# A decoder layer with 32 experts on one core: one expert's weights go where the residual rows lay, and the embedding rows take a way through memory

## What is computed

```
mix = (sigmoid(ga) * branch_a + sigmoid(gb) * branch_b) @ w_out
x = layer_norm(DN_ALPHA * x + mix, ln1_g, ln1_b)
ffn = hier_moe(x)          # best of 4 groups, 2 best of its 8 experts; SwiGLU experts
x = layer_norm(DN_ALPHA * x + ffn, ln2_g, ln2_b)
ple = sigmoid(x @ w_ple_gate) * (p @ w_ple_proj)
x = x + rms_norm(ple, ple_norm_g)
```

## Time and profile before

| what | us |
|---|---|
| median of 3 runs | 960.75 |
| lowest, highest | 960.75, 961.34 |
| profiled execution | 960.12 |
| its span | 958.3 |

### The profile page before, as it was taken

One profiled execution on the slowest core, in us unless ns is written; L12 is line 12 of the kernel. 1 busy time (PEld: TensorE's weight loads), 2 busy tenths in 40 slices (PEclk: granted clock), 3 DMA queues, 4 the chain that ended last, 5 costly groups with the idle time before them and its releaser, 6 DMA issues.

```text
span 958.3 us, 14059 instructions
## 1 busy us (share of the span) xinstructions
PE 918.7 (96%) x5317; PEld 553.9 (58%) x5317; DVE 425.0 (44%) x979; ACT 249.0 (26%) x538; POOL 96.8 (10%) x146
## 2 busy tenths in 40 slices
PE   8999999999999999999999999989999889987997
PEld 7777777777777766565678744444333323333444
DVE  0311467767734228777642243682111211113784
ACT  1122222032145015566740011131111101111346
POOL 0111211211221200000000000011121111110000
PEclk9999999999999999999999999999999999999999
DMA  9876888998797802011024794349999999998601
GB/s 374 346 250 233 283 289 316 328 334 302 275 349 273 291 23 69 28 39 42 21 80 154 307 425 171 150 164 345 419 423 423 421 427 423 424 418 352 250 23 66
DMA packets 65418, 247.52 MB, mean 258 GB/s; under 512 B 11301, under 2 KB 12078, under 8 KB 56358
## 3 DMA queue, kind: packets, MB, share of 16 engines
q1 hardware_dynamic: 46742, 191.41, 51.4%
q0 software_dynamic: 13216, 35.28, 10.1%
q10 hardware_dynamic: 5392, 19.93, 5.6%
HBM read 240.98 MB, written 18.05 MB: 270 GB/s over the span
## 4 chain that ended last, share of the span: by engine, by line
PE 76%; DMA 12%; DVE 6%; ACT 2%; issue 2%; SPq 1%; DVEq 0%; ACTq 0%
PE ps L895 21%; DMA arena<-in_wexp 10%; PE ps L1365 8%; PE ps L1285 6%; PE ps L1216 4%; PE ps L1490 3%; PE ps L1387 3%; PE ps L983 3%; PE ps L954 3%; PE ps L1068 3%; PE ps L886 3%; PE ps L1092 2%; PE ps L1032 2%; PE ps L1049 1%; PE ps L958 1%
## 5 line engine op out<-in xcount | busy, mean ns | idle before, releaser
L895 PE MATMUL ps<-arena 128*128 128x260 f32 x928 | 214.3, 386 | 1.7 <-DMA arena<-in_xT 1.4
L895 PEld LDWEIGHTS ps<-arena 128*128 128x128 f32 x928 | 172.7, 190 | 36.7 <-issue 8.8
L1874 DVE SCALAR_TENSOR_TENSOR arena<-arena,vec 128x512 f32<-128x512 f32 x120 | 81.7, 745 | 0.0
L2556 POOL DMA_DIRECT2D arena<-in_kv x96 | 51.7, 539 | 264.4 <-issue 258.3
L1387 PE MATMUL ps<-arena 128*64 128x512 f32 x288 | 67.8, 614 | 5.3 <-DMA arena<-in_wexp 5.3
L1365 PE MATMUL ps<-arena 128*64 128x512 f32 x288 | 65.4, 607 | 6.9 <-DMA arena<-in_wexp 5.8
L1365 PE MATMUL ps<-arena,con 128*64 128x512 f32 x288 | 63.8, 595 | 2.9 <-DMA arena<-in_wexp 2.9
L2381 DVE TENSOR_TENSOR arena<-ps,arena 128x256 f32<-128x256 f32 x18 | 7.6, 424 | 125.4 <-ACT arena L1725 125.4
L1285 PE MATMUL ps<-arena 128*128 128x512 f32 x128 | 58.0, 600 | 0.0
L1387 PEld LDWEIGHTS ps<-arena 128*64 128x64 f32 x288 | 22.1, 142 | 48.3 <-issue 48.3
L1216 PE MATMUL ps<-arena 128*128 128x260 f32 x224 | 49.3, 382 | 0.0
(11 more groups left out here) (360 smaller groups left out, 1196.4 us busy)
## 6 DMA issues: line engine op xcount, KB each, us to landing
arena<-in_wexp SPq DMA_DIRECT2D x26, 2048.0 KB, 25.2
arena<-in_kv SPq DMA_DIRECT2D x160, 272.0 KB, 9.2
arena<-in_wexp SPq DMA_DIRECT2D x36, 1024.0 KB, 27.3
arena<-in_kv POOLq DMA_DIRECT2D x96, 272.0 KB, 7.5
arena<-in_w ACTq DMA_DIRECT2D x35, 512.0 KB, 7.3
arena<-in_wexp SPq DMA_DIRECT2D x16, 512.0 KB, 9.5
arena<-in_wo SPq DMA_DIRECT2D x8, 512.0 KB, 3.3
arena<-in_w_out SPq DMA_DIRECT2D x4, 1024.0 KB
```

The source lines that it names most:

```text
L895: y = mm(ps[:, b + h, 0:TH], w[:, k], xT[:, k, h * TH:(h + 1) * TH], start=(k == 0), stop=(k == KD - 1))
L1874: y = v.scalar_tensor_tensor(out=aT[:, c, 0:NPR], in0=win, scalar=wt, in1=aT[:, c, 0:NPR], op0=ALU.mult, op1=ALU.add)
L2556: pool.dma_start(rec[:, n % 2, SPN + j], a["kv"][bass.ds(pg, 1)].rearrange("a p n -> (a p) n")).then_inc(s_kvp[n % 2], 16)
```

## The change

1. Expert 31 can no longer have two blocks (its threshold in CTWO becomes unreachable), so it keeps place 31. Its weights get a place of their own, `wlast`, over `x1` and what lies behind it. They come in six pieces: row tiles 3 and 2 when their embedding rows are stored; then, behind the wait for R_IDS and for the first row gather, the down part, tile 1's and tile 0's place. TensorE takes them in pass 17. The pairwise loads of load 15 become loads of one expert.
2. The projected embedding rows are stored to memory by ScalarE (`ple_store`), the last tile behind the copy of the first gathered rows. SP loads them back near the end (`load_embedding`), and `pgr` with them.
3. The last tile of the output projection runs half by half, and VectorE adds and takes statistics of each half as it is there.
4. `ids` is computed on 32 partitions and read by SP in two single loads; `cmp8`, `ovc`, `idc` move.

The diff, cut (the rest adjusts counts of semaphores):

```
-        cmp8 = at(A_X1T, 256).rearrange("p (e m) -> p e m", m=8)
+        cmp8 = at(A_LATE, 256).rearrange("p (e m) -> p e m", m=8)
...
-        ovc = at(A_X1T, 512).rearrange("p (b e) -> p b e", b=16)[0:1]
-        plc = at(A_X1T, 1024).rearrange("p (b e) -> p b e", b=32)[0:1]
-        ids = pages[0:1, 0:NEXP]
+        ovc = at(A_PLT, 512).rearrange("p (b e) -> p b e", b=16)[0:1]
+        plc = at(A_LATE + 256, NEXP)[0:NEXP]
+        ids = decay[0:NEXP, 0:1].bitcast(I32)
 
         idx = sb("idx", [P, NPB + 2], U32)
         idy = sb("idy", [P, NPB + 2], U32)
-        idc = sb("idc", [P, 5], U32)
+        idc = lsum[:, 0:5].bitcast(U32)
+        wlast = at(A_WLAST, EW)
...
+        pld = nc.dram_tensor("embedding_scratch", (T, D), F32, kind="Internal").ap()
...
+        s_wl, WL0 = s_wo[0], 16 * KD // 2
+        s_ps = [(s_x[0], 16), (s_x[1], 16), (s_x[2], 16), (s_x[3], 16), (s_wo[1], 16 * KD // 2)]
+        s_pl = [(s_pw[0], 64), (s_pw[1], 64), (s_rw[0], 32), (s_rw[1], 32), (s_wq, 32)]
...
+            def last_expert(lo, hi):
+                sp.dma_start(wlast[:, lo:hi], a["wexp"][NEXP - 1, :, lo:hi]).then_inc(s_wl, 16)
+
+            for u in range(1, TILES - 2):
+                sp.wait_ge(s_ps[u][0], s_ps[u][1] + 16)
+                last_expert(ORDER[u] * D, (ORDER[u] + 1) * D)
             sp.wait_ge(s_r, R_IDS)
+            sp.wait_ge(s_xg[0], 16)
+            sp.wait_ge(s_ps[0][0], s_ps[0][1] + 16)
+            last_expert(EW1, EW)
+            for u in range(TILES - 2, TILES):
+                sp.wait_ge(s_ps[u][0], s_ps[u][1] + 16)
+                last_expert(ORDER[u] * D, (ORDER[u] + 1) * D)
 
             def gate_up_weights(k):
                 n = numbers[2 * (k % 3):2 * (k % 3) + 2]
-                sp.load(n, ids[0:1, 2 * LOAD_ORDER[k]:2 * LOAD_ORDER[k] + 2])
+                for x in range(2):
+                    sp.load(n[x:x + 1], ids[2 * LOAD_ORDER[k] + x:2 * LOAD_ORDER[k] + x + 1, 0:1])
...
-                        for x in range(2):
-                            sp.dma_start(wx[k % 3][:, x, lo:hi], a["wexp"][bass.ds(e[x], 1), :, lo:hi].rearrange("a p n -> (a p) n")
-                                         ).then_inc(s_half if half else s_wx[k % 3], 16)
+                        sp.dma_start(wx[k % 3][:, 0, lo:hi], a["wexp"][bass.ds(e[0], 1), :, lo:hi].rearrange("a p n -> (a p) n")
+                                     ).then_inc(s_half if half else s_wx[k % 3], 16)
 
             def down_weights(k):
                 n = numbers[2 * (k % 3):2 * (k % 3) + 2]
                 sp.wait_ge(m.y, LAST_USE[k - 3] + 1)
-                for x in range(2):
+                for x in range(2 if k < EPAIRS - 1 else 1):
...
-            sp.dma_start(pgr[:], a["lnrows"][:, 4]).then_inc(s_plw, 16)
...
+            def load_embedding(u):
+                t = ORDER2[u]
+                sp.dma_start(x1[0:ROWS[t], t], pld[t * P:t * P + ROWS[t]]).then_inc(s_pl[u][0], 16)
+
+            sp.wait_ge(s_plw, 64)
+            load_embedding(0)
+            sp.dma_start(pgr[:], a["lnrows"][:, 4]).then_inc(s_plw, 16)
+            load_embedding(1)
+            load_x(3)
+            load_results(3)
+            load_embedding(2)
+            load_x(4)
+            load_results(4)
+            load_embedding(3)
+            load_embedding(4)
...
+                last = u == TILES - 1
+                for n in range(2 * KD):
+                    h, k = divmod(n, KD) if last else (n % 2, n // 2)
+                    if u == 2 and n in (2, 4, 6):
+                        (turn_x1, logits_x1, turn_logits)[n // 2 - 1](0)
+                    if u >= 2 and n in (8, 10, 12):
+                        (turn_x1, logits_x1, turn_logits)[n // 2 - 4](u - 1)
+                    y = mm(ps[:, b + h, :], mixT[:, k, t * P:(t + 1) * P], wbig[:, k, h * 512:(h + 1) * 512],
+                           start=(k == 0), stop=(k == KD - 1))
+                    if last and n == KD - 1:
+                        y.then_inc(s_f0, 1)
...
+            def expert_of(p, slot, x):
+                return wlast if isinstance(p, int) and p == NPASS - 1 and x == 1 else wx[slot][:, x]
+
+            def loaded_of(k):
+                return 32 * (k // 3 + 1) - (16 if k == EPAIRS - 1 else 0)
+
             def gate_up(p, slot, loaded, turned):
+                if isinstance(p, int) and p == NPASS - 1:
+                    pe.wait_ge(s_wl, WL0 + 16 * TILES)
...
+            def ple_store(u):
+                t = ORDER[u]
+                act.wait_ge(s_ppe, u + 1)
+                act.dma_start(pld[t * P:t * P + ROWS[t]], x1[0:ROWS[t], t]).then_inc(s_ps[u][0], 16)
+
             x1_out_last()
             logits_out(TILES - 1)
             ple_out(0)
+            ple_store(0)
 
             act.wait_ge(s_r, R_EXP)
             av(gg[:], gx[:], ACT.Exp).then_inc(s_ra, 1)
@@ -1715,6 +1767,8 @@
             av(gf, gf, ACT.Exp).then_inc(s_ra, 1)
             for u in range(1, TILES):
                 ple_out(u)
+                if u < TILES - 1:
+                    ple_store(u)
...
             rows_in(0, 0)
+            ple_store(TILES - 1)
...
+                if u == TILES - 1:
+                    for hh in range(2):
+                        if hh == 0:
+                            dve.wait_ge(s_f0, 1)
+                        else:
+                            dve.wait_ge(s_f, TILES)
+                        q = x[:, hh * 512:(hh + 1) * 512]
+                        v.scalar_tensor_tensor(out=q, in0=q, scalar=ALPHA, in1=ps[:, b + hh, :],
+                                               op0=ALU.mult, op1=ALU.add).then_inc(s_fd, 1)
+                        dve.wait_ge(s_fd, FD * u + 2 * hh + 1)
+                        v.bn_stats(bst[:, hh], q).then_inc(s_fd, 1)
+                    break
...
-            step(v.tensor_tensor(plc, place[0:1].unsqueeze(1).to_broadcast([1, NEXP, NEXP]),
-                                 con[0:1, CEID:CEID + NEXP].unsqueeze(2).to_broadcast([1, NEXP, NEXP]), ALU.is_equal))
-            step(v.tensor_tensor(plc, plc, con[0:1, CEID:CEID + NEXP].unsqueeze(1).to_broadcast([1, NEXP, NEXP]), ALU.mult))
-            step(v.tensor_reduce(shift[0:1], plc, AX.X, ALU.add))
-            step(v.tensor_copy(ids, shift[0:1]))
+            step(v.scalar_tensor_tensor(out=plc, in0=place[0:NEXP], scalar=con[0:NEXP, CPART:CPART + 1],
+                                        in1=con[0:NEXP, CEID:CEID + NEXP], op0=ALU.is_equal, op1=ALU.mult))
+            step(v.tensor_reduce(shift[0:NEXP, 0:1], plc, AX.X, ALU.add))
+            step(v.tensor_copy(ids, shift[0:NEXP, 0:1]))
...
+                dve.wait_ge(s_pl[u][0], s_pl[u][1] + 16)
                 v.tensor_tensor(q, q, x1[0:n, t], ALU.mult).then_inc(s_pm, 1)
                 dve.wait_ge(s_pm, u + 1)
                 if u >= 1:
                     dve.wait_ge(s_fy, u)
+                else:
+                    dve.wait_ge(s_plw, 80)
...
-    con[:, CTWO:CTWO + 32] = np.where(np.arange(32) < FIXED, BIG, CAP)
+    con[:, CTWO:CTWO + 32] = np.where((np.arange(32) < FIXED) | (np.arange(32) == NEXP - 1), BIG, CAP)
```

More of the change, by code:

```diff
@@ L134 @@
 R_EARLY = 39
-R_EXP, R_EXP2, R_RANK, R_IDX, R_IDS, R_STEPS = 43, 48, 51, 74, 78, 92
+R_EXP, R_EXP2, R_RANK, R_IDX, R_IDS, R_STEPS = 43, 48, 51, 74, 77, 91
 LOGITS_READ = {2: 2, 3: 4, 4: 17}
@@ L230 @@
 assert A_W2 + 2 * EW == A_X1
+A_WLAST = A_X1
+A_LATE = A_WLAST + EW
+assert A_WLAST + EW1 == A_X1 + (TILES - 1) * D and A_LATE + 256 + NEXP == A_W0
 A_XG = A_MIX
@@ L704, in store_x1 @@
                 t = ORDER[u]
[L705 removed]
+                sp.wait_ge(s_fd, FD * (u + 1) + (3 if u == TILES - 1 else 0))
                 for k in range(2):
@@ L819, in _ @@
                 load_gate(k)
-            for u in range(3, TILES):
-                load_x(u)
-                load_results(u)
+            def load_embedding(u):
[12 more added lines that the diff above has]
+            load_embedding(4)
             for u, t in enumerate(ORDER2):
@@ L1278, in _ @@
                     pe.wait_ge(s_fd, FD * (u - 2) + 1)
-                for k in range(KD):
-                    if u == 2 and k in (1, 2, 3):
-                        (turn_x1, logits_x1, turn_logits)[k - 1](0)
-                    if u >= 2 and k in (4, 5, 6):
-                        (turn_x1, logits_x1, turn_logits)[k - 4](u - 1)
-                    for h in range(2):
-                        y = mm(ps[:, b + h, :], mixT[:, k, t * P:(t + 1) * P], wbig[:, k, h * 512:(h + 1) * 512],
-                               start=(k == 0), stop=(k == KD - 1))
+                last = u == TILES - 1
[9 more added lines that the diff above has]
+                        y.then_inc(s_f0, 1)
                 y.then_inc(s_f, 1)
@@ L1409, in _ @@
                     slot, n = weight_slot(PASS[p - 1][1])
-                    down(p - 1, slot, 32 * n)
+                    down(p - 1, slot, loaded_of(PASS[p - 1][1]))
                 if p + 2 < NPASS:
@@ L1428, in _ @@
             slot, n = weight_slot(EPAIRS - 1)
```

(6 more changed lines are left out.)

32 lines of the change are left out of this document (17 added, 15 removed).

## The result

The changed kernel takes 964.04 us in the median of 9 runs (961.64 to 964.83); the kernel before, run beside it, takes 961.51 (9 runs, 960.03 to 962.75). The ratio is 1.0026, 95% interval 1.0016 to 1.0036: slower by 2.5 us. The forecast was 958.7 with a range to 963.0, so the time lies above the range, 1.5 us from what rival 1 (the store comes late) gives.

A forecast was written before the change was run, and what follows sets the result against it. The expert weight stream (DMA full, 655 to 847 us) was taken to set the pace. -1.38 + 0.7 - 1.30 = -2.0 us against the profiled 960.12 gave 958.1, or 958.7 from the runs' median; range 955.5 to 963.0.

The forecast's parts named there:

- rival 1: Last embedding store lands after 7.3 us, load 3 starts 5.7 late: +1.8, 962.5 us; decides from 5.5 on; chance 0.15.
- The store's landing: ScalarE's last embedding store, ahead of load 3, lands 3.5 us after issue (median of L707's stores), at 649.1.
- The stream's start: Load 3, head of the expert weight stream, starts at 650.4 instead of 648.49, 1.9 us late.
- From start to end: Load 14's landing: load 3's 1.9 us late start less 1.24 us for pgr, net +0.7 us.
- The last weights: TensorE's wait before pass 16's down product goes, as expert 31 leaves the queue ahead of it: -1.38 us.
- `pgr`, -1.24: The half-mebibyte row of the norm's gains leaves the weight stream ahead of load 14: -1.24 us.
- The branch: TensorE's 6.54 us branch over the overflow loop waits for code behind data; idle engines then shorten it: -1.30 us.
- rival 2: The lighter queue gives nothing at TensorE's overflow branch, its 6.54 us being queued matmuls: 960.0 us; chance 0.20.
- The early pieces: Expert 31's pieces ahead of the first gather are done by 639, with 0.8 us of cover: no cost.
- The half tiles: Output projection's last tile in halves: VectorE's statistics end at 617.5 instead of 617.9, gain 0.4 us, no own term.
- Routing steps, ScalarE's stores, the end: Shorter routing steps, store issues of about 0.35 us each, and 2.6 MB more loaded at the end change nothing.
- rival 5: Expert 31 gets more than 64 rows, so an overflow pass runs, 14.9 us: 975 us; chance 0.01.

The follow-up runs named there:

- a_store_alone: Changed kernel, but SyncE waits for the last embedding store first and only then issues the three pieces behind the gather; 960.07 us, one run.
- b_late3: Kernel before, with the first three quarters of load 3 issued only behind pass 0's gate/up product; 965.5 us, ratio 1.0045.
- a_defer: Changed kernel with expert 31's last row block and SyncE's wait for tile 0's store moved behind load 3 and expert 5's second half; 958.7 us, ratio 0.998.
- b_pgr: Kernel before with only the load of pgr (the last norm's gains) moved to the end; 959.71 us, ratio 0.9978.
- b_pgr_warm: b_pgr with nine instead of five idle TensorE products behind the last passes; 960.9 us, ratio 0.9998.
- b_emb: b_pgr with the embedding rows also stored and loaded back near the end, expert 31 as before; 959.26 us, ratio 0.9965.
- a_nobranch: Changed kernel without TensorE's part of the overflow passes and its branch over them; 962.2 us, ratio 1.0011.
- a_last: Changed kernel with tile 0's piece of expert 31 and SyncE's wait for its store moved right ahead of load 15; 958.34 us, ratio 0.9967.
- a_three_late: Changed kernel with expert 31's down part, tile 1's and tile 0's pieces right ahead of load 15, SyncE's gather wait dropped; 960.36 us, ratio 0.9981.
- a_quiet: Changed kernel; expert 31: tile 3's piece before the gather, tile 2's and down part behind, tiles 1 and 0 before load 15; tile 1's store later; 958.38 us.
- b_front: Kernel before with only the output projection's last tile in halves and ids on 32 partitions with two single register loads; 961.28 us, ratio 0.9991.

## Why the prediction was wrong, step by step

**The store's landing: the step that failed.** "The nearest rows for a half-mebibyte store are those of L707 ... I take the median", 3.5 us, with the reason that the one and a half mebibyte "need 3.7 us and have mostly passed". Measured: 7.6 us. The pieces had not passed, and the store was behind a queue: SyncE issues them only behind the landing of the first gather, 1.2 us before the store's issue. I had worked out their 3.7 us of transfer and then set the store after it without writing down when they start. They go out from 644.50 on, so by that same 3.7 us they are through at 648.2 at the earliest, and the store is beside them for its whole way. They and the store are 2 mebibyte, 5.0 us at 422 GB/s, so to 649.5. The loads ran slower than that (219 GB/s from 648 to 650, with next to nothing of the store among it), and the store, last in line, moved its data from 649.6 on and landed at 653.3. Why the loads were slow there isn't shown; in `a_store_alone`, from 650 to 651 us and with the store long landed, the first of them run no faster (213 GB/s). The value from ScalarE's own loads in a full queue, 7.3, was the nearer row. The Trainium skill (DMA: Bandwidth & Descriptors, section 🔬 Queues, rings and completion order), named in the prediction, has a semaphore land only after every earlier write of that DMA engine across its queues. The two landings don't contradict it, but the trace has another reason for most of the 7.6 us: the store's data themselves moved late. Alone, its packets run from 646.4 to 648.0; beside the loads from 649.6 to 653.0, and from there to the landing only 0.3 us are left for a semaphore that this rule would hold back.

**The stream's start.** Forecast 650.4, measured 654.78. Of the 4.4 us between them 4.1 are the store's. The two register loads and the rest from the last piece's issue (653.3) to load 3 take 1.5 us instead of the 1.3 that I had, and the single loads are the cheaper ones (0.28 against 0.47).

**From start to end.** That load 14 is late by what load 3 is late held: +5.6 at pass 16, and b_late3 shows the same slope without the change. Rival 1 used it, and its place and its price (7.3 for 7.6) were right; its turning point (5.5) lies between the landings measured, 2.6 and 7.6, and no run tests it more closely. It gave 962.5 and 964.0 was measured. In the profiled executions it came to +3.5 where it said +1.8: -1.30 for the branch came as -0.5 (0.8 of the difference), the start was 6.3 late rather than 5.7 (0.6), and the rest is within what the dips move. I gave it 0.15; by the order of issues alone it was the likeliest case.

**The last weights, -1.38: right, as far as the wait goes.** No wait stands before 870.82, and in a_defer none before 865.66, while b_pgr keeps its 1.33.

**`pgr`, -1.24: right in sign by b_pgr,** 2.1 (1.2 to 3.2); its variant b_pgr_warm shows no gain (-0.8 to 1.2).

**The branch, -1.30: a wrong premise.** "the engines are idle at the branch" didn't hold. Its rows in the changed kernel, by source line (ns; first and last start), against the earlier trace rows, and a window over it:

```profile
L617 ACTq COMPARE_BRANCH  x1: 58/58/58, 880.8 to 880.8; - x1
L617 PEldq COMPARE_BRANCH  x1: 6016/6016/6016, 882.0 to 882.0; - x1
```

```profile
875.00:885.00 10.00, 9.09 (x33) 4.13 (x33) 5.25 (x8) 2.64 (x5) 2.34 (x2) 1.00 1.01 389
```

It still takes 6.0 us, and the DMA share there is 1.01: SyncE issues the results of tile 0 (L801) only at 872.51, in before at 869.50, behind a scatter issued at 865.23, and the gate weights behind them, so these fill the engines just then. I had let them go earlier because the stream ends earlier, without writing out what they wait for. Gained were 0.5 us. A lighter queue isn't seen to help: over the thirteen traced kernels that have the branch it takes 5.85 to 6.54 us, and 6.08 in b_emb, where the engines' share during it is 0.84 and not 0.98 or more. That products queued in front are all of it, as rival 2 has it, doesn't hold either: in the changed kernel the last of them ends at 885.59 and the branch at 888.0. For code there is a sign. In each of the thirteen, one packet of the queue that the profile names q8 instruction moves during the branch (in the changed kernel between 885 and 886 us), and a_nobranch has none from 860 to 900. Whether the branch waits for it, and whether a truly idle queue would shorten it, wasn't tried.

**The early pieces.** "the pieces ahead of it are done by 639": the second is issued at 638.18 and lands 4.8 us later, at about 643 (they wait for stores that I had landed sooner), and the gather issued at 640.67 lands after 3.78 us, so TensorE stands 2.01 us before its transposes (where the earlier trace rows had none) and pass 0's product takes 8.78. In the changed kernel this costs nothing at load 3, since SyncE waits longer for the store; with that wait gone it is the next thing late, as load 3 at 652.83 and 651.74 in the profiles of a_last and a_three_late against 647.71 in a_quiet's shows. In the medians it doesn't stand out.

**The half tiles, -0.4: right.** Half a tile and its statistics in the changed kernel, with the aggregation behind them (VectorE's timeline), and then the aggregation of before:

```profile
614.30 0.69 DVE L2294 SCALAR_TENSOR_TENSOR arena<-arena,ps 128x512 f32<-128x512 f32 x1
615.02 0.69 DVE L2297 BATCH_NORM_STATS2 bst<-arena 128x6 f32<-128x512 f32 x1
...
617.06 0.21 DVE L2323 BATCH_NORM_AGGREGATE mv<-bst 128x2 f32<-128x12 f32 x1
```

```profile
617.91 0.21 DVE L2259 BATCH_NORM_AGGREGATE mv<-bst 128x2 f32<-128x12 f32 x1
```

The aggregation starts 2.39 us after TensorE turns to its next product (614.67), where in before it was 2.75 (615.16 to 617.91).

**Routing steps, ScalarE's stores, the end: nothing, right.** VectorE's first product with embedding rows (906.97) has no wait in front of it, and b_front and b_emb show no price. The engines are not idle there, though: from 905 to 907 us their share is 1.02, where the earlier trace rows had 0.03.

**What the range left out.** It ended at 963.0, at the half of rival 1. The ends of the store's landing (2.6 to 12.9) had been worked out as -0.2 to +10.1 us for load 14, and I cut that end off by a chance instead of by a reason. A slip without weight: rival 5's 975 is 960.75 + 14.9 = 975.6.

## What to carry to other kernels

A wait in an issue list that is worked off in order costs everything behind it. Before a wait is put into such a list, look at what stands behind it: if it is the head of a transfer stream that is full to its end, each microsecond by which the engines stand for it is nearly one of the kernel's (0.7 to 0.9 here), and a filler that needs a wait belongs behind the stream's head, not in front. Price a store by what is issued beside it in the microseconds before, with start times written out, not by the median of its kind. Bytes taken out of a full stream pay only up to the last block that someone waits for, or so the sum had it; no run here isolates it.

## What the hardware showed that I had not expected

- A store of half a mebibyte lands 2.6 us after its issue with no load issued beside it, and 7.6 us after it with 1.5 mebibyte of loads issued from another queue in the 1.2 us before. Its first packet moves about 3 us later than alone: the loads go first, although they stand on another queue.
- TensorE's compare-and-branch over the overflow loop takes 6.0 and 6.5 us in after and before, and 5.85 to 6.54 over all kernels that have it, where ScalarE's takes 0.058.
- The dips of the granted clock fall at other places from profile to profile and move a 7.09 us product to 8.67 or 8.78, and 12.3 to 13.95. Executions of one kernel spread over 2.1 to 5.7 us. In the kernel before their mean granted clock runs from 0.985 to 0.994, and the longer ones tend to have the lower clock (correlation -0.5 to -0.7 in three batches of 23 to 29), so the dips are a part of the spread, not all of it.
- Two register loads of one number each, 0.28 us apiece in the median, are hardly dearer than one of two numbers (0.47).
